# The low parts of two weight units of a fused decoder block, on GpSimd instead of VectorE

## What is computed

```python
h = _rmsnorm(x, norm_mix_g)
a_val, a_gate, b_in = split(h @ w_in, [512, 1024])
ya = silu(_layernorm(_causal_dwconv(a_val * sigmoid(a_gate), conv_a_w, conv_a_b), ln_a_g, ln_a_b))
# pooling: group g has the window w = 2, 4, 8, 16
d = (trailing sum of b_in over w tokens) / min(position, w) - b_in
yb = (d @ pool_w[g]) * pool_scale
x = x + concatenate([ya, yb]) @ w_out
h = _rmsnorm(x, norm_ffn_g)
gate, val = split(h @ w_up, 2)
x = x + (silu(_causal_dwconv(gate, conv_f_w, conv_f_b)) * val) @ w_down
out = _rmsnorm(x, norm_final_g)
```

## Time and profile before

| | |
|---|---|
| median of 3 runs | 1035.25 us (1035.09 to 1037.4) |
| the profiled execution's own time | 1034.48 us |
| its span | 1032.7 us |
| TensorE matmul busy | 978.9 us, 95% |
| VectorE busy | 531.0 us, 51% |
| ScalarE busy | 311.7 us, 30% |
| GpSimd busy | 155.6 us, 15% |
| mean granted clock of TensorE | 0.983 |

### The profile page before, as it was taken

How to read it: one execution, slowest core, us unless ns; L and a number is a source line. 1 busy time by engine, 2 the same in 40 slices (tenths; PEclk the granted TensorE clock), 3 DMA queues, 4 the chain that set the end, 5 groups by cost and what they waited for, 6 DMA issues and landing times.

```text
span 1032.7 us, 10774 instructions
## 1 busy us (share of the span) xinstructions
PE 978.9 (95%) x4370; PEld 809.6 (78%) x4370; DVE 531.0 (51%) x547; ACT 311.7 (30%) x386; POOL 155.6 (15%) x132
## 2 busy tenths in 40 slices
PE   4999986679999999999999999999999999999997
PEld 3888765457888888888888888888888888888885
DVE  5699899658443434344353442533524335243157
ACT  7473673362523321220212202122022221221114
POOL 3378698642000000000000000000000000000000
PEclk9999998889999999999999999999999999999999
DMA  7302101131002302112021120211102111130004
GB/s 279 98 26 82 41 1 41 42 126 59 1 1 82 122 1 82 42 56 67 1 82 41 42 77 4 81 41 41 55 26 81 41 41 42 40 102 1 1 1 163
DMA packets 37125, 58.03 MB, mean 56 GB/s; under 512 B 1082, under 2 KB 30266, under 8 KB 37085
## 3 DMA queue, kind: packets, MB, share of 16 engines
q1 hardware_dynamic: 37088, 57.53, 16.2%
HBM read 53.33 MB, written 4.19 MB: 56 GB/s over the span
## 4 chain that ended last, share of the span: by engine, by line
PE 85%; DVE 8%; ACT 2%; POOL 2%; issue 1%; DMA 1%; SPq 0%; POOLq 0%; DVEq 0%; ACTq 0%
PE slot L1059 84%; DVE slot L773 4%; POOL conv L425 2%; PE slot L1085 1%; DVE w_lo L745 1%; DVE tmp L730 1%; ACT prod L544 1%; DMA x_sb<-in_x 1%; DVE act_lo L737 0%; DVE tokens L812 0%; ACT tmp L458 0%; ACT w_hi L473 0%; DVE conv L784 0%; DVE act_lo L840 0%; DVE bn L825 0%
## 5 line engine op out<-in xcount | busy, mean ns | idle before, releaser
L1059 PE MATMUL slot<-act_hi,w_hi 128*128 128x512 f32 x896 | 350.2, 391 | 2.3 <-DVE x_sb L798 1.8
L1059 PE MATMUL slot<-act_lo,w_hi 128*128 128x512 f32 x896 | 349.3, 390 | 0.0
L1059 PE MATMUL slot<-act_hi,w_lo 128*128 128x512 f32 x896 | 349.1, 390 | 0.0
L1059 PEld LDWEIGHTS slot<-act_hi,w_hi 128*128 128x128 f32 x896 | 168.8, 188 | 37.6 <-DVE x_sb L798 2.2
L1059 PEld LDWEIGHTS slot<-act_hi,w_lo 128*128 128x128 f32 x896 | 168.6, 188 | 35.3
L1059 PEld LDWEIGHTS slot<-act_lo,w_hi 128*128 128x128 f32 x896 | 168.6, 188 | 34.8
L997 DVE TENSOR_TENSOR x_sb<-x_sb,slot 128x1024 f32<-128x1024 f32 x88 | 107.4, 1221 | 99.4 <-PE slot L1059 99.0
L635 ACT ACTIVATE w_hi<-raw 128x1024 fp32r<-128x1024 f32 x66 | 68.5, 1054 | 282.9 <-PE slot L1059 282.9
L973 DVE SCALAR_TENSOR_TENSOR tmp<-slot,fchan,tmp 128x1023 f32<-128x1023 f32 (+1 forms) x44 | 56.4, 1282 | 188.9 <-ACT tmp L686 186.9
L1059 PE MATMUL slot<-w_hi,gv_hi 128*128 128x512 f32 x352 | 136.9, 389 | 0.0
L1059 PE MATMUL slot<-w_lo,gv_hi 128*128 128x512 f32 x352 | 136.9, 389 | 0.0
(11 more groups left out here) (84 smaller groups left out, 632.9 us busy)
## 6 DMA issues: line engine op xcount, KB each, us to landing
raw<-in_w_up SPq DMA_DIRECT2D x22, 1024.0 KB, 5.0
raw<-in_w_down SPq DMA_DIRECT2D x11, 1024.0 KB, 4.9
x_sb<-in_x SPq DMA_DIRECT2D x12, 512.0 KB, 8.8
raw<-in_w_in SPq DMA_DIRECT2D x6, 1024.0 KB, 5.1
raw<-in_w_out SPq DMA_DIRECT2D x4, 1024.0 KB, 5.0
out<-raw SPq DMA_DIRECT2D x8, 512.0 KB, 2.6
gain<-in_norm_mix_g SPq DMA_DIRECT2D x1, 512.0 KB, 5.2
gain<-in_norm_ffn_g SPq DMA_DIRECT2D x1, 512.0 KB, 4.3
```

What stands on the lines that cost most here:

```text
L1059: mm = nc.tensor.matmul(out_ap, st[s], mv[v], start=first and s == v == 0, stop=last and s == 1)
```

## The change

Units 6 and 7, the first two of `w_out`, get their low parts from GpSimd (`half_lo`) and no longer from VectorE (`unit_lo`). On GpSimd the two halves of unit 6 stand ahead of `windows(3, ...)`, those of unit 7 behind `windows(2, ...)`. `half_lo` learns the layout of row units. The counts of the semaphores follow: `POOL_UNITS` and `DVE_UNITS` list who makes which unit, `dve_half` counts VectorE's halves, and the sync queue (`load_unit`) and TensorE (`unit_ready`) wait on the semaphore of the engine that makes the unit.

```diff
--- before.py
+++ after.py
@@ -104,13 +104,17 @@
 
         return 0 if isinstance(i, int) and i == CHUNKS - 1 and kind == "d" else "gvd".index(kind)
 
-    POOL_UNITS = 3
+    POOL_UNITS = (0, 1, 2, 6, 7)
+    DVE_UNITS = (3, 4, 5, 8, 9)
 
     def half_count(q, t):
 
-        return 2 * t + q + 1 if q < 2 else 2 * q + t + 1
-
-    HI0, LO0 = 2 * U_FFN, 2 * (U_FFN - POOL_UNITS)
+        return 2 * t + q + 1 if q < 2 else 2 * POOL_UNITS.index(q) + t + 1
+
+    def dve_half(q, t):
+        return 2 * DVE_UNITS.index(q) + t + 1
+
+    HI0, LO0 = 2 * U_FFN, 2 * len(DVE_UNITS)
 
     def ffn_half(kind, i, t):
 
@@ -293,8 +297,8 @@
 
             def load_unit(q):
 
-                if q >= 2 + POOL_UNITS:
-                    sp.wait_ge(lo_done, 2 * (q - 2 - POOL_UNITS) + 2)
+                if q - 2 in DVE_UNITS:
+                    sp.wait_ge(lo_done, dve_half(q - 2, 1))
                 elif q >= 2:
                     sp.wait_ge(lo_pool_done, half_count(q - 2, 1))
                 if q < U_OUT:
@@ -386,9 +390,10 @@
             def half_lo(q, t):
 
                 s = W_SLOT[q]
-                pool.wait_ge(hi_done, half_count(q, t))
-                nc.gpsimd.tensor_tensor(half_of(w_lo[s][:, :], True, t), half_of(raw[:, q % 2, :], True, t),
-                                        half_of(w_hi[s][:, :].bitcast(F32), True, t),
+                columns = q < U_OUT
+                pool.wait_ge(hi_done, 2 * t + q + 1 if q < 2 else 2 * q + t + 1)
+                nc.gpsimd.tensor_tensor(half_of(w_lo[s][:, :], columns, t), half_of(raw[:, q % 2, :], columns, t),
+                                        half_of(w_hi[s][:, :].bitcast(F32), columns, t),
                                         ALU.subtract).then_inc(lo_pool_done, 1)
 
             def windows(g, before):
@@ -438,8 +443,12 @@
             light_taps(2, 0)
             light_taps(1, 1)
             light_taps(3, 0)
+            half_lo(6, 0)
+            half_lo(6, 1)
             windows(3, 0)
             windows(2, WINDOW_STEPS[3])
+            half_lo(7, 0)
+            half_lo(7, 1)
             light_taps(2, 1, 1, 8)
             windows(1, WINDOW_STEPS[2])
             light_taps(2, 1, 8)
@@ -896,14 +905,12 @@
             conv_taps((3, 0, 20))
             conv_join(1, 1)
             conv_taps((2, 1, 6))
-            unit_lo(6)
             conv_join(3, 0)
             conv_taps((2, 1, 5))
             pool_difference(3)
             ln_stats(0)
             conv_taps((2, 1, 6))
             pool_difference(2)
-            unit_lo(7)
             conv_taps((3, 1, 6))
             ya_lo(0)
             difference_lo(0)
@@ -1105,13 +1112,17 @@
 
             order = [(2 * (j // 2) + b, j % 2) for j in range(CT) for b in range(2)] + [(4, 1), (4, 0), (5, 1), (5, 0)]
 
+            def unit_ready(q, t):
+
+                if q in POOL_UNITS:
+                    pe.wait_ge(lo_pool_done, half_count(q, t))
+                else:
+                    pe.wait_ge(lo_done, dve_half(q, t))
+
             def in_projection(n):
                 q, t = order[n]
                 slot_read(J_IN[n])
-                if q < POOL_UNITS:
-                    pe.wait_ge(lo_pool_done, half_count(q, t))
-                else:
-                    pe.wait_ge(lo_done, 2 * (q - POOL_UNITS) + t + 1)
+                unit_ready(q, t)
                 column_tile(slot_of(J_IN[n]), W_SLOT[q], t)
 
 
@@ -1171,7 +1182,7 @@
 
                     made = ("ya", m // HT, CT - 1) if r < 2 else ("yb", 2 * r - 3)
                     pe.wait_ge(act_lo_done, DONE[made])
-                    pe.wait_ge(lo_done, 2 * (q - POOL_UNITS) + 2)
+                    unit_ready(q, 1)
                     for kk in range(2):
                         for h in range(2):
                             mm = three_passes(slot_of(n)[:, bank[h]], [a[:, k0 + kk, cols] for a in act],
```

## The result

The changed kernel takes 1038.70 us (median of 10 runs, 1037.26 to 1039.74), the kernel before 1035.08 (10 runs). Forecast were +2.3 and the range 1035.0 to 1039.8, so the time lies in the range, but on the slower side, which had 0.25. The profiled execution of the changed kernel has a span of 1037.1 and an own time of 1038.90.

A forecast was written before the change was run, and what follows sets the result against it. TensorE, busy 95%, was taken as the bound, with pool_product(1)'s end at 201.7 the date that matters. GpSimd's delay of pool_difference(1), +4.0 less 1.8 slack, gave +2.3: 1036.8 profiled, 1037.5 median, range 1035.0 to 1039.8.

The forecast's parts named there:

- the slower side: Whole kernel slower by over 0.3%: TensorE's clock falling before pool_product(1), or slower hand-overs between engines; chance 0.25.
- rival A: GpSimd's halves are cheap, 1.90 each instead of 2.40: total +0.1 to +0.3, so 1035.5; chance 0.17.
- The slack of 1.8: On ScalarE ahead of pool_output(0): pool_difference(1) may come 1.8 later before ScalarE feels it; beyond that each microsecond counts.
- steps 1 to 3: Unit 6, unit 7 and windows(1) on GpSimd: pool_difference(1) +4.0, less slack, so pool_product(1) starts 2.3 later.
- the string: Serial chain from pool_product(1)'s end at 201.7 through pool_output(1), taps, windows(0) and pool_difference(0) to yb_lo(1): shifted by 2.3.
- Step 2: Unit 7 on GpSimd delays a tap, so ScalarE's product 9 and Silu: ya_lo(0) at 188.3 against 188.03, VectorE's 6.8 gone.
- step 4: Everything behind pool_product(1): unchanged but shifted, TensorE's 9.2 wait stays, nothing behind 217 swallows the shift; sum +2.3.
- Rival B: TensorE idles some 2.2 before pool_product(1), its clock falls and the six matmuls take twice 1.4: +3.7, 1038.9; chance 0.25.
- the room up to +4.5: Upper end of the range: hand-overs between engines 0.1 to 0.2 slower on each of the dozen pieces on the path.

The follow-up runs named there:

- e10: Changed kernel plus zero matmuls on TensorE, 38 ahead of pool_product(2) and six behind it: median 1037.05 us.
- e9: Kernel before plus zero matmuls on TensorE, 38 ahead of pool_product(2) and six behind it: median 1035.21 us.
- e3: Changed kernel with ScalarE's light_products(2, 1, 8, 10) moved behind ln_silu(0): median 1038.51 us.
- e4: Changed kernel with the first half of unit 7 ahead of windows(2) on GpSimd instead of behind it: median 1038.83 us.
- e11: Kernel before plus three unused bn_stats on VectorE ahead of yb_lo(1), a pure delay of 1.8: median 1038.94 us.
- e12: Kernel before plus six unused bn_stats on VectorE ahead of yb_lo(1), a pure delay of 3.6: median 1038.02 us.
- e1: Changed kernel with unit 7 back on VectorE, so only unit 6 moves to GpSimd: median 1035.99 us, ratio to before 1.0008.

## Why the prediction was half right

**Right, with sizes.** A half on GpSimd: 2.40 taken, 2.34 measured, so rival A (1.90) falls. pool_difference(3): +0.6 said, +1.0 measured (+0.8 counted from A), since windows(3) undisturbed takes 8.8 and not 8.4: its last sum is 2.37 even with VectorE idle, and I had put all above 1.89 down to VectorE. First tap of (2, 1): start at 179.15 said, 178.26 measured. That the seven taps end at 188.9 as said is luck: they start 0.9 earlier and take 0.9 longer (10.62 for 9.7), since VectorE's pieces of pool_difference(2) fell among the taps and not between the halves. ya_lo(0): 188.3 said, 188.80 measured. pool_difference(1): done at 198.6 said, 198.50 measured, +3.9 for +4.0. The slack of 1.8 swallowed its part: pool_output(0) at 199.8 said, 199.50 measured. pool_output(1): +2.3 said, +2.1 measured, 203.80. The sum of steps 1 to 3 is the string, +2.3 said, +1.9 measured from A, and e10 against e9 gives it as a difference in time, 1.84 (1.3 to 2.8).

**Wrong in its reason.** Step 2 put ya_lo(0)'s date down to the product that waits in ScalarE's queue: "VectorE's 6.8 are gone here: it waits for ScalarE". The wait is there, but e3 takes it away and ya_lo(0) does not move. VectorE's relief was eaten by its own queue: conv_join(3, 0)'s early start was lost in the wait of 4.07 for windows(3), and unit 7's 3.45 in pool_difference(2), which takes 5.8 instead of 2.65 as its pieces wait for GpSimd's second half and two taps. I had counted what this exclusion costs GpSimd, 1.15 for VectorE's main piece between the halves, which did not come (the two took 4.68), and not what it costs VectorE: 2.33 for an instruction of seven elements. The Trainium skill, SBUF — State Buffer, section "SBUF: two separate sides", has the exclusion last for the whole instruction of whoever is first; by that rule, the trace agrees: a piece of 7 elements took 2.33 in the changed kernel and one of 15 elements 2.33 in e4, the length of a half.

**The step that failed** is step 4: "From there the string to yb_lo(1) and on is what it was, shifted." It is not. TensorE restarts behind the 9.2 wait at half clock, and stays there for 3.3 in the profiled execution of before and for 8.3 in that of the changed kernel. The sum lacked a term, 2.3 in the profiled execution (13.83 less 11.56). In the medians the change costs 3.6, and with the clock held on both sides 1.84 (e9 to e10), which leaves some 1.8 for it, or 0.8 to 2.3 by the spread of that difference. e11 shows that this term comes with a delay alone, with no work moved; the profiled executions of e12 and e1 show that it does not grow with the delay and can come with almost none. Rival B had the clock as its cause, but ahead of pool_product(1), where the trace of the changed kernel shows 1.00; the loss of the clock lies behind yb_lo(1). So the slower side came true by a mechanism at another place than B's. That the time lies in the range is in part luck: the room up to +4.5 was there for hand-overs slower than taken, and what filled it was this term.

**Open.** The pieces B to C of the fourteen traces fall into two groups, 11.56 to 11.60 (six, four of them with filled gaps) and 13.18 to 14.43 (eight), and nothing lies between. That the changed kernel's runs mostly had the late return of the clock, and before's mostly the early one, is inferred from their medians, one profile each and, for before, the mean clocks given with e11 and e12; how often each comes in a kernel was not counted. What makes the return late in one execution and early in another with the same restart is not shown. e1 warns of it: its profile has the longer piece, its median is nearly that of before.

## What to carry to other kernels

Moving work to an idle engine is free only if nobody listens to what is queued behind it there: here the idle engine's string carried the date, and the relieved engine was made to wait by the very instructions it had handed over, through operands both take from SBUF. Count that exclusion on both sides, and by the whole length of the instruction that is met. Where TensorE waits long, a shift of its restart is worth its own length plus or minus what the clock does; filling the wait and the small gaps behind it with matmuls on zeros separates the string's price from the clock's. Here it gave back 1.7 of the changed kernel's 3.6, and nothing in the kernel before.

## What the runs showed of the hardware

- The granted clock behind a wait of 9.2 came back 3.3 after TensorE's restart in before's profiled execution, 8.3 after it in the changed kernel's and 9.6 in e1's, with the same matmuls. A pure delay of 3.6 was no dearer than one of 1.8 (+3.0 and +3.9). The Trainium skill, TensorE: Matmul & The Clock Gate, section "What's actually happening", says that the date of the change depends on where the first matmul falls in a schedule of the chip's own, which does not begin with the kernel; before and e1 agree, with restarts at 213.6 and 213.7 and full clock at 216.9 and 223.3.
- On GpSimd, the sum of a tile and itself shifted by 1, 2 or 4 elements takes 1.89 for some 1020, but shifted by 8 it takes 2.37 (163.39 in the changed kernel, VectorE idle, and 2.36 or 2.37 in the five other traces that have unit 6 on GpSimd), as much as a subtraction of two different tiles (2.34).
- A low part of 8 pieces of 128 and one of 1024 in one piece cost GpSimd the same: mean 2.40 and 2.34.
